# A hybrid decoder block on one core: expert rows added into the residual by the scatter, the last expert placed by TensorE, the gate matmul of the tail in split form, and the down bias and the per-layer embedding computed ahead of the experts

## The chip, the core and the metric

The kernel runs on one core of one Trainium2 chip. A core has TensorE (PE: matmuls, and PEld: its weight loads), VectorE (DVE), ScalarE (ACT), GpSimd (POOL) and SyncE (SP), and 16 DMA engines that all of them share. The metric is the device time of one execution in microseconds (us); lower is better. Times of a trace are counted from the start of the profiled span.

## The reference, cut to what matters

One decoder block over 512 tokens of width 1024 in float32: a mixer (not touched), then a mixture of experts (4 of 32 experts for each token), then a gated per-layer embedding and a final norm.

```python
# the mixture of experts, for each token t and its 4 experts e with softmax weights w
gu = h[t] @ w_gate_up[e] + b_gate_up[e]
gate, up = split(gu)            # clamped to 7
act = (up + 1) * gate * sigmoid(1.702 * gate)
out[t] += w * (act @ w_down[e] + b_down[e])

x = x + out
ple_gate = sigmoid(rms_norm(x, ple_norm_g) @ w_ple_gate)     # 1024 x 1024
x = x + ple_gate * (p @ w_ple_proj)                          # 256 x 1024
return rms_norm(x, final_norm_g)
```

## The kernel before, in words

The program is written out engine by engine, with semaphores between the engines; nothing is scheduled by a tool. It has three parts, which the trace puts at 0 to 660 us (the mixer), 660 to 1887 us (routing and 32 experts) and 1887 to 1996 us (the tail).

**Split matmuls.** A float32 product is made of three matmuls in the type fp32r: each operand is written as a high part (an ACT copy that rounds) and a low part (a DVE subtraction), and high x high, low x high and high x low are summed in PSUM. Plain float32 matmuls are used in the tail and for small products; each of them stands in the trace as two rows.

**Routing.** PE computes the logits (L1697), DVE picks the top 4 and builds one-hot rows, PE ranks the tokens of each expert (L1704, L1707). Then a loop over the 32 experts turns ranks into slots: DVE compares (L1398), PE multiplies the one-hot block with token numbers (L1801). The result is `tok_idx` (which token sits in slot s of expert e) and `dst_idx` (its row in the buffer `y_rows` of 2048 rows, one for each token and choice). While this loop runs, ACT makes the high parts of the first three weight chunks (L1023), and the DMAs of `wpg`, the 4 MB of gate weights, run (L1009).

**Experts.** Weights come as 12 chunks of 1 MB for each expert, by SP, into a ring of 6 buffers; a slot is loaded again when DVE has made its low part (L593, L600). Split parts have 3 buffers. For each expert POOL gathers the rows of its tokens from `h_rows` by an indirect DMA (L742), PE turns them (L1715), ACT and DVE split them into `xgT_h`, `xgT_l`; PE adds the gate/up bias by four short matmuls (L1720), multiplies 8 chunks into `gu_ps` (L1729, L1733), then adds the down bias by two matmuls (L1720, `down_bias`) and multiplies 4 chunks into `dn_ps` (L1744, L1749). ACT copies `dn_ps` into `y_sb` (L1035) and POOL scatters it into `y_rows` (L754). POOL's order in the loop is: wait for PE's turning, gather the rows of the expert three ahead, wait for `y_sb`, scatter, wait until the scatter has landed, and free `y_sb`.

**Passes.** After the 32 experts each engine runs through `passes` (L497), a loop that reads the largest expert's row count from SBUF three times, and would repeat the experts if one had more than 128 rows. None has here.

**Tail.** SP loads `p`, `w_ple_proj`, the residual `x1_rows` and the final gain, and after POOL's `moe_end` the 16 tiles of `y_rows` (L638). PE turns `p` and multiplies the embedding (L1835, L1842). For each of 4 blocks of 128 tokens DVE adds four weighted expert rows to the residual (L1499), ACT and DVE compute the norm (L1094, L1105, L1096, L1490), DVE scales the rows (L1504), PE turns them (L1855), DVE applies the gain (L1507), PE multiplies by the gate weights in plain float32 (L1862), ACT applies the sigmoid (L1091, L1092), DVE multiplies and adds (L1514, L1515), and a second norm gives the output rows (L1519), which SP stores (L641).

## Time and profile before

| what | us |
|---|---|
| runs: median of 3 (lowest to highest) | 2001.38 (2000.07 to 2005.04) |
| the profiled execution, device time | 1997.68 |
| its span in the trace | 1996.0 |
| PE busy in the span | 1879.9 (94%) |
| DVE busy | 1436.4 (72%) |
| ACT busy | 1154.7 (58%) |
| POOL busy | 301.8 (15%) |
| DMA moved | 512.41 MB, mean 257 GB/s |

Busy time is a share of the whole span; the stages differ. A granted TensorE clock of 1.00 in a stretch means 2.4 GHz throughout, 0.50 means 1.2 GHz throughout. A row of the timeline has the start in us, the length in us, the engine, the line, the operation, the tiles (output <- inputs), the count of merged instructions, and in brackets how long the engine had been idle and what ended that. Matmul rows overlap by their pipeline, so that the pace is read from one start to the next, not from the lengths.

### The profile page before, as it was taken

To read this page: it belongs to the slowest core of one execution; us is meant where nothing else is said; L and a number is where in the kernel's file an instruction comes from. 1 tells how busy PE (TensorE), PEld (TensorE's weight loads), DVE (VectorE), ACT (ScalarE), POOL (GpSimd) and SP (SyncE) were. 2 spreads that over 40 slices of the span, in tenths; PEclk is the share of its full clock that TensorE was granted. 3 is DMA by queue.
4 is the path that set the end of the run, shared out by engine and by line. 5 is a ranking of instruction groups with operands and counts; after the bars stand their busy time and mean duration, and the time that the engine had idled before them with its cause. 6 is when DMAs were issued, how large, how long until landed. Compare 5 with 4: busy or idle time off the path is not lost.

```text
span 1996.0 us, 25440 instructions
## 1 busy us (share of the span) xinstructions
PE 1879.9 (94%) x9038; PEld 1520.5 (76%) x9038; DVE 1436.4 (72%) x1021; ACT 1154.7 (58%) x898; POOL 301.8 (15%) x267
## 2 busy tenths in 40 slices
PE   6999998989999668999999999999999999999787
PEld 5788887768879556888888888888888888888633
DVE  3576585553341557898898988988889888898545
ACT  4555554242231236777777777777777777777423
POOL 5133323610000010111011110110101101010000
PEclk9999999999999678999999999999999999999989
DMA  5334434143364247999999999999999999999550
GB/s 171 104 105 117 108 119 114 56 132 97 94 196 174 105 184 279 357 367 369 361 364 362 371 365 366 371 366 376 362 363 371 358 370 367 359 369 357 195 210 38
DMA packets 155559, 512.41 MB, mean 257 GB/s; under 512 B 14964, under 2 KB 75028, under 8 KB 121876
## 3 DMA queue, kind: packets, MB, share of 16 engines
q1 hardware_dynamic: 141860, 482.26, 65.8%
q0 software_dynamic: 11520, 25.19, 4.2%
q10 hardware_dynamic: 2128, 4.26, 0.6%
q8 instruction: 34, 0.56, 0.1%
q14 instruction: 17, 0.14, 0.0%
HBM read 502.15 MB, written 26.28 MB: 265 GB/s over the span
## 4 chain that ended last, share of the span: by engine, by line
PE 81%; DVE 7%; ACT 5%; issue 3%; POOL 3%; DMA 1%; SPq 0%; DVEq 0%; ACTq 0%; POOLq 0%
PE gu_ps L1729 23%; PE gu_ps L1733 12%; PE dn_ps L1744 12%; PE gu_ps L1541 6%; PE gu_ps L1542 6%; PE gu_ps L1543 6%; PE dn_ps L1749 6%; PE et_ps L1715 3%; PE gu_ps L1862 2%; PE gu_ps L1720 1%; ACT w_hi L799 1%; POOL win L726 1%; PE gu_ps L1560 1%; PE gu_ps L1842 1%; PE dn_ps L1720 1%
## 5 line engine op out<-in xcount | busy, mean ns | idle before, releaser
L1427 DVE TENSOR_TENSOR split_l<-ring,split_h 128x2048 fp32r<-128x2048 f32 x384 | 871.6, 2290 | 133.9 <-ACT split_h L1023 129.6
L1023 ACT ACTIVATE split_h<-ring 128x2048 fp32r<-128x2048 f32 x384 | 731.1, 1917 | 187.6 <-PE gu_ps L1733 144.6
L1729 PE MATMUL gu_ps<-split_h,xgT_h 128*128 128x512 f32 x1024 | 285.1, 400 | 0.7 <-DVE xgT_l L1433 0.7
L1729 PE MATMUL gu_ps<-split_h,xgT_l 128*128 128x512 f32 x1024 | 275.9, 391 | 0.0
L1733 PE MATMUL gu_ps<-split_l,xgT_h 128*128 128x512 f32 x1024 | 274.8, 390 | 0.0
L1729 PEld LDWEIGHTS gu_ps<-split_h,xgT_l 128*128 128x128 f32 x1024 | 193.4, 189 | 41.3
L1733 PEld LDWEIGHTS gu_ps<-split_l,xgT_h 128*128 128x128 f32 x1024 | 193.1, 189 | 40.8
L1729 PEld LDWEIGHTS gu_ps<-split_h,xgT_h 128*128 128x128 f32 x1024 | 191.1, 189 | 41.7 <-DVE xgT_l L1433 1.6
L1111 DVE TENSOR_TENSOR w_lo<-w_raw,w_hi 128x2048 fp32r<-128x2048 f32 (+1 forms) x45 | 106.1, 2358 | 152.7 <-ACT w_hi L799 152.6
L1744 PE MATMUL dn_ps<-split_h,actT_h 128*128 128x512 f32 x512 | 167.7, 409 | 1.9 <-DVE actT_l L1433 1.9
L739 POOL COPY icur<-tok_idx 128x1 int32 (+1 forms) x32 | 39.9, 1247 | 800.7 <-PE et_ps L1715 757.7
L1744 PE MATMUL dn_ps<-split_h,actT_l 128*128 128x512 f32 x512 | 159.2, 392 | 0.0
L1541 PE MATMUL gu_ps<-hT_h,w_hi 128*128 128x512 f32 x392 | 154.9, 395 | 0.0
L1542 PE MATMUL gu_ps<-hT_l,w_hi 128*128 128x512 f32 x392 | 153.0, 390 | 0.0
L1543 PE MATMUL gu_ps<-hT_h,w_lo 128*128 128x512 f32 x392 | 152.9, 390 | 0.0
L1749 PE MATMUL dn_ps<-split_l,actT_h 128*128 128x512 f32 x512 | 137.2, 390 | 0.0
L799 ACT ACTIVATE w_hi<-w_raw 128x2048 fp32r<-128x2048 f32 (+1 forms) x45 | 85.0, 1889 | 59.6 <-PE gu_ps L1543 53.2
L1744 PEld LDWEIGHTS dn_ps<-split_h,actT_l 128*128 128x128 f32 x512 | 96.7, 189 | 20.8
L1749 PEld LDWEIGHTS dn_ps<-split_l,actT_h 128*128 128x128 f32 x512 | 96.3, 188 | 20.5
L1744 PEld LDWEIGHTS dn_ps<-split_h,actT_h 128*128 128x128 f32 x512 | 94.5, 190 | 22.7 <-DVE actT_l L1433 2.4
L1541 PEld LDWEIGHTS gu_ps<-hT_h,w_hi 128*128 128x128 f32 x392 | 74.1, 189 | 15.5 <-issue 0.6
L1543 PEld LDWEIGHTS gu_ps<-hT_h,w_lo 128*128 128x128 f32 x392 | 73.8, 188 | 15.5
(252 smaller groups left out, 2546.0 us busy)
## 6 DMA issues: line engine op xcount, KB each, us to landing
ring<-in_w_gate_up SPq DMA_DIRECT2D x256, 1024.0 KB, 7.0
ring<-in_w_down SPq DMA_DIRECT2D x128, 1024.0 KB, 7.5
w_raw<-in_w_in SPq DMA_DIRECT2D x28, 1024.0 KB, 5.8
arow<-acum_rows POOLq DMA_DIRECT2D x16, 512.0 KB, 6.6
w_raw<-in_w_ssd_out SPq DMA_DIRECT2D x8, 1024.0 KB, 5.7
yr<-y_rows SPq DMA_DIRECT2D x16, 512.0 KB, 10.4
w_raw<-in_w_in SPq DMA_DIRECT2D x9, 512.0 KB, 6.6
w_raw<-in_w_mix_out SPq DMA_DIRECT2D x4, 1024.0 KB, 8.8
```

Source lines behind the costliest of these rows:

```text
L799: a.activation(w_hi[HI_SLOT[n]][:, 0:size], w_raw[RAW_SLOT[n]][:, 0:size], ACT.Copy).then_inc(w_high, 1)
L1023: a.activation(split_h[s % SPLIT][:, :], ring[s % RING][:, :], ACT.Copy).then_inc(hi_done, 1)
L1111: v.tensor_tensor(w_lo[RAW_SLOT[n]][:, 0:size], w_raw[RAW_SLOT[n]][:, 0:size], w_hi[HI_SLOT[n]][:, 0:size].bitcast(F32), ALU.subtract).the ...
L1427: v.tensor_tensor(split_l[s % SPLIT][:, :], ring[s % RING][:, :], split_h[s % SPLIT][:, :].bitcast(F32), ALU.subtract).then_inc(lo_done, 1)
L1541: o = t.matmul(pb(key)[:, cols], sh, mh, start=n == 0, stop=False)
L1542: o = t.matmul(pb(key)[:, cols], sh, ml, start=False, stop=False)
L1543: o = t.matmul(pb(key)[:, cols], sl, mh, start=False, stop=n == len(parts) - 1)
L1715: o = t.transpose(et_ps[:, k * P:k * P + P], blocks[:, k * P:k * P + P], ident[:, :])
L1729: t.matmul(gu_ps[:, b * 512:b * 512 + 512], x[:, k, :], split_h[s][:, b * 512:b * 512 + 512], start=False, stop=False)
L1733: o = t.matmul(gu_ps[:, b * 512:b * 512 + 512], xgT_h[:, k, :], split_l[s][:, b * 512:b * 512 + 512], start=False, stop=k == KD - 1)
L1744: t.matmul(dn_ps[:, b * 512:b * 512 + 512], x[:, 2 * r + k, :], split_h[s][:, k * DM + b * 512:k * DM + b * 512 + 512], start=False, stop= ...
L1749: o = t.matmul(dn_ps[:, b * 512:b * 512 + 512], actT_h[:, 2 * r + k, :], split_l[s][:, k * DM + b * 512:k * DM + b * 512 + 512], start=Fal ...
```

## The change

1. **The scatter adds.** The DMA of POOL adds the rows of `y_sb` to `x1_rows`, the residual in DRAM, instead of writing them to `y_rows`. The routing weight is applied earlier, as the scale of ACT's copy into `y_sb`: the slot loop now yields the weight of each slot (`wslot`) beside the token, and POOL copies the next expert's column into `wcur` (`weigh`). `y_rows`, its loads and the 16 weighted additions in the tail are gone.
2. **The last expert** isn't scattered: its product stays in `dn_ps`, is scaled and split (`y_h`, `y_l`), and is placed by matmuls with a 0/1 matrix (`place`, slot against token) and added to the residual on DVE.
3. **The gate matmul of the tail** takes split operands: the weights with the norm's gain folded in (`wpg_h`, `wpg_l`), the unnormed rows (`x2T_h`, `x2T_l`), and the norm's factor becomes the scale of the sigmoid. The order is by k, so that the first block can start before all weights are split; the last block of 128 tokens is finished in two halves.
4. **The down bias** leaves the experts: `share3` holds each token's weight for each of the 32 experts, and share x `b_down` is added to the residual `X` once, by `add_bias`, after the slot loop. The stores of `x1_rows` wait for that.
5. **The embedding** p x w_ple_proj is computed between the routing's steps and in `add_bias`; its inputs are loaded during the last block of the mixer.

```diff
+                if c == CH - 1:
+                    wait_proj(sp, ("MO", c, 1))
+                    sp.dma_start(prow[:, :, :], p[0, 0].rearrange("(c p) d -> p c d", p=P)).then_inc(p_loaded, 16)
+                    sp.dma_start(pj[:, :, :], w_ple_proj[0].rearrange("(k p) f -> p k f", p=P)).then_inc(p_loaded, 16)
+                    for m in range(3):
+                        sp.dma_start(bdown[m * NE:m * NE + NE, :], b_down[0]).then_inc(bd_loaded, 16)
                 sp.dma_start(h_rows[c * P:c * P + P, :], h2[:, c, :]).then_inc(rows_stored, 16)
-                sp.dma_start(x1_rows[c * P:c * P + P, :], X[:, c, :]).then_inc(rows_stored, 16)
-
-            sp.wait_ge(rows_stored, 16 * 2 * CH)
+            sp.wait_ge(rows_stored, 16 * CH)
+            for c in range(CH):
+                sp.wait_ge(bd_added, c + 1)
+                sp.dma_start(x1_rows[c * P:c * P + P, :], X[:, c, :]).then_inc(x1_stored, 16)
             weights(0, RING)
...
-            sp.dma_start(prow[:, :, :], p[0, 0].rearrange("(c p) d -> p c d", p=P)).then_inc(p_loaded, 16)
-            sp.dma_start(pj[:, :, :], w_ple_proj[0].rearrange("(k p) f -> p k f", p=P)).then_inc(p_loaded, 16)
-            for c in range(CH):
-                sp.dma_start(x2[c][:, :], x1_rows[c * P:c * P + P, :]).then_inc(x2_loaded[c], 16)
             sp.dma_start(ogain[:, :], final_norm_g.partition_broadcast(P)).then_inc(ogain_loaded, 16)
             sp.wait_ge(moe_end, 1)
             for c in range(CH):
-                rows = y_rows[c * ROWS // CH:(c + 1) * ROWS // CH, :].rearrange("(p k) d -> p k d", k=TOPK)
-                for k in range(TOPK):
-                    sp.dma_start(yr[c][:, k, :], rows[:, k, :]).then_inc(yr_loaded[c][k], 16)
-            for c in range(CH):
-                sp.wait_ge(o_done, c + 1)
...
+            def scatter(n, col, steps, following=None):
                 pool.wait_ge(y_evac, n + 2)
                 alone(pool)
+                if following is not None:
+                    weigh(following)
...
-                g.indirect_dma_start(out=y_rows, out_offset=bass.IndirectOffsetOnAxis(ap=dcur[:, 0:1], axis=0),
+                g.indirect_dma_start(out=x1_rows, out_offset=bass.IndirectOffsetOnAxis(ap=dcur[:, 0:1], axis=0),
+                                     in_=y_sb[:, :], in_offset=None, bounds_check=SEQ - 1,
+                                     oob_is_err=False, compute_op=ALU.add
                                      ).then_inc(y_stored, 16)
...
-            act.wait_ge(rows_stored, 16 * 2 * CH)
-            for h in range(2):
-                act.dma_start(wpg[h][:, :, :], wpg_v[:, :, h * 512:h * 512 + 512]).then_inc(pg_loaded, 16)
+            for k in range(0, KD, 4):
+                act.dma_start(wpg[:, k:k + 4, :], wpg_v[:, k:k + 4, :]).then_inc(pg_loaded, 16)
+            embed(0)
+            act.wait_ge(share_done, 1)
+            act.wait_ge(bd_loaded, 16 * 3)
+            a.activation(bstk[:, :], bdown[:, :], ACT.Copy).then_inc(b_high, 1)
+            act.wait_ge(share_turned, 1)
+            a.activation(shareT[:, :], bank[4][0:3 * NE, :], ACT.Copy).then_inc(share_high, 1)
+            embed(1)
+            act.wait_ge(rows_stored, 16 * CH)
...
-                a.activation(y_sb[:, :], dn_ps[:, :], ACT.Copy).then_inc(y_evac, 1)
+                act.wait_ge(w_ready, n + 1)
+                a.activation(y_sb[:, :], dn_ps[:, :], ACT.Copy, scale=wcur[:, 0:1]).then_inc(y_evac, 1)
...
+                if isinstance(j, int):
+                    for i in range(2, 2 * CH):
+                        embed(i)
...
-            def down_bias(n, e):
+            def down_free(n):
 
                 pe.wait_ge(y_evac, n + 1)
-                for b in range(2):
-                    bias(dn_ps[:, b * 512:b * 512 + 512], e, 2 * DM + b * 512)
 
...
+            def add_bias():
...
+                pe.wait_ge(share_low, 1)
+                pe.wait_ge(slots_done, 2)
+                for c in range(CH):
+                    if c >= 2:
+                        pe.wait_ge(bd_added, c - 1)
+                    ps = dn_ps if c % 2 == 0 else et_ps
+                    for h in range(2):
+                        o = t.matmul(ps[:, h * 512:h * 512 + 512], shareT[:, c * P:c * P + P],
+                                     bstk[:, h * 512:h * 512 + 512], start=True, stop=True)
+                    o.then_inc(bd_mm, 1)
+                    embed(4 + c)
+                pe.wait_ge(pp_read, 2 * CH + 1)
+                pe.wait_ge(bd_added, CH)
+
...
+            t.transpose(et_ps[:, 0:P], ident[:, :], ident[:, :]).then_inc(last_mm, 1)
+
+            def put_back(c):
...
+                for h in range(2):
+                    pe.wait_ge(y_low, h + 1)
+                    for n, part in enumerate((y_h, y_l)):
+                        o = t.matmul(tail_b[c][:, h * 512:h * 512 + 512], place[:, c * P:c * P + P],
+                                     part[:, h * 512:h * 512 + 512], start=n == 0, stop=n == 1)
+                o.then_inc(back_mm, 1)
...
+            def gate(c, k, h):
+
+                if c == 0 and h == 0:
+                    pe.wait_ge(pg_low, k + 1)
+                ps = bank[2 * ((c + 1) % 2) + h]
+                for n, (a, b) in enumerate(((x2T_h, wpg_h), (x2T_l, wpg_h), (x2T_h, wpg_l))):
+                    o = t.matmul(ps[:, :], a[c % 2][:, k, :], b[:, k, h * 512:h * 512 + 512],
+                                 start=k == 0 and n == 0, stop=k == KD - 1 and n == 2)
+                return o
...
```

Where the rows stand now. **ACT between the exponential of the routing and the first expert.** Before (`split_h` is the high part of a weight chunk, `xgT_h` the turned rows):

```order
L1002 ACTIVATE rt_78<-rt_78 128x16 [waits route_in]
L1009 DMA wpg_187<-in_w_ple_gate 128x8x512 [waits rows_stored,logits_mm]
L1009 DMA wpg_188<-in_w_ple_gate 128x8x512
L1023 ACTIVATE split_h_167<-ring_161 128x2048 [waits chunk_used,e_loaded0]
L1023 ACTIVATE split_h_168<-ring_162 128x2048 [waits chunk_used,e_loaded1]
L1023 ACTIVATE split_h_169<-ring_163 128x2048 [waits chunk_used,e_loaded2]
L1015 ACTIVATE xgT_h<-et_ps 128x1024 [waits et_done]
```

Now (`pp` is a half block of the embedding, `bstk` the bias, `shareT` the turned weights of the tokens):

```order
L1047 ACTIVATE rt_77<-rt_77 128x16 [waits route_in]
L1058 DMA wpg<-in_w_ple_gate 128x4x1024 [waits logits_mm]
L1058 DMA wpg<-in_w_ple_gate 128x4x1024
L1052 ACTIVATE pp<-gu_ps 128x512 [waits pp_mm]
L1062 ACTIVATE bstk<-bdown 96x1024 [waits bd_loaded,share_done]
L1064 ACTIVATE shareT<-et_ps 96x512 [waits share_turned]
L1052 ACTIVATE pp<-gu_ps 128x512 [waits pp_mm]
L1080 ACTIVATE split_h_166<-ring_160 128x2048 [waits chunk_used,e_loaded0,rows_stored]
L1080 ACTIVATE split_h_167<-ring_161 128x2048 [waits chunk_used,e_loaded1]
L1080 ACTIVATE split_h_168<-ring_162 128x2048 [waits chunk_used,e_loaded2]
L1052 ACTIVATE pp<-gu_ps 128x512 [waits pp_mm] x6
L1072 ACTIVATE xgT_h<-et_ps 128x1024 [waits et_done]
```

The first three high parts stand behind `shareT` now, which waits for PE's turning after the slot loop; before, only the DMA issues stood between them and the exponential.

**DVE between the slot loop and the first expert's rows.** Now; before, the three `split_l` stood right behind the slot sums, and `xgT_l` right behind them:

```order
L1512 TENSOR_TENSOR wslot<-rt_78,dn_ps 128x32 [waits slot_step]
L1581 TENSOR_TENSOR bstk<-bdown,bstk 32x1024 [waits b_high]
L1584 TENSOR_TENSOR shareT<-et_ps,shareT 32x512 [waits share_high]
L1529 TENSOR_TENSOR split_l_169<-ring_160,split_h_166 128x2048 [waits hi_done]
L1529 TENSOR_TENSOR split_l_170<-ring_161,split_h_167 128x2048 [waits hi_done]
L1529 TENSOR_TENSOR split_l_171<-ring_162,split_h_168 128x2048 [waits hi_done]
L1546 TENSOR_TENSOR X<-X,dn_ps 128x1024 [waits bd_mm]
L1546 TENSOR_TENSOR X<-X,et_ps 128x1024 [waits bd_mm]
L1546 TENSOR_TENSOR X<-X,dn_ps 128x1024 [waits bd_mm]
L1546 TENSOR_TENSOR X<-X,et_ps 128x1024 [waits bd_mm]
L1535 SCALAR_TENSOR_TENSOR xgT_l<-et_ps,xgT_h 128x1024 [waits et_hi]
```

Four additions to the residual `X` have come in between the low parts and the rows of the first expert.

**PE after the last expert.** Now (`et_ps<-ident` is a turning whose only use is to mark that PE has come this far; before, the first row here was the turning of `p`, behind the same branch):

```order
L1914 MATMUL dn_ps<-split_l_171,actT_h 128x512 x3
L529 UNCONDITIONAL_BRANCH
L527 REGISTER_ALU
L527 COMPARE_AND_BRANCH
L2021 MATMUL et_ps<-ident 128x128
L2032 MATMUL gu_ps<-y_h,place 128x512 [waits y_low,placed]
L2032 MATMUL gu_ps<-y_l,place 128x512
L2032 MATMUL gu_ps<-y_h,place 128x512 [waits y_low]
L2032 MATMUL gu_ps<-y_l,place 128x512
```

The mark on which ACT's `y_h` waits stands behind the loop `passes`, not in front of it.

## Rows read from the trace of the kernel before

**Rows 1.** Windows: span, busy us (count) of PE, PEld, DVE, ACT, POOL, clock, DMA.
```profile
679.00:705.00 26.00, 17.91 (x127) 13.18 (x127) 20.54 (x31) 1.83 (x2) 0.00 (x0) 0.50 0.31 114
1000.00:1200.00 200.00, 200.00 (x932) 162.64 (x931) 177.61 (x90) 148.21 (x90) 27.27 (x24) 1.00 0.96 365
```

**Rows 2.** Timeline of PE where one expert's gate/up chunks end.
```profile
887.99 1.07 PE L1733 MATMUL gu_ps<-split_l,xgT_h 128*128 128x512 f32 x4
888.90 0.61 PE L1720 MATMUL dn_ps<-bparts,sel 96*128 96x512 bf16 x2
889.15 0.82 PE L1744 MATMUL dn_ps<-split_h,actT_h 128*128 128x512 f32 x2
889.81 0.62 PE L1744 MATMUL dn_ps<-split_h,actT_l 128*128 128x512 f32 x2
```

**Rows 3.** Groups of DVE from 800 to 1840 us: busy, mean ns, idle before.
```profile
L1427 DVE TENSOR_TENSOR split_l<-ring,split_h 128x2048 fp32r<-128x2048 f32 x349 | 792.1, 2290 | 103.6 <-ACT split_h L1023 99.8
```

**Rows 4.** DMA view, 1000 to 1200 us: totals; issues with us to landing.
```profile
DMA packets 14027, 72.94 MB, mean 365 GB/s; under 512 B 2029, under 2 KB 2029, under 8 KB 8220
...
ring<-in_w_gate_up SPq DMA_DIRECT2D x44, 1024.0 KB, 7.0
...
y_rows<-y_sb,dcur POOLq DMA_INDIRECT x6, 7.7
```

**Rows 5.** DMA view, 800 to 850 us: GB/s in 40 slices.
```profile
GB/s 226 285 347 331 374 367 213 328 318 246 377 439 433 400 413 413 419 413 419 380 269 413 341 400 351 305 419 324 419 387 338 403 384 416 282 282 387 252 393 383
```

**Rows 6.** Timeline of POOL in one expert: gather's copy, scatter's issue.
```profile
896.18 1.28 POOL L739 COPY icur<-tok_idx 128x1 int32 x1 [24.46 <-PE et_ps L1715]
...
906.51 1.01 POOL L754 DMA_INDIRECT y_rows<-y_sb,dcur  x1 [0.88 <-POOL dcur L751]
```

**Rows 7.** Timeline from the logits to the first expert's second chunk.
```profile
661.76 3.60 PE L1697 MATMUL et_ps<-wr,h2T 128*128 128x32 f32 x16 [0.78 <-ACT h2T L999]
...
668.76 1.04 DVE L1365 TENSOR_REDUCE chosen<-oh 128x128 f32<-128x512 f32 x1
...
674.14 1.89 PE L1707 MATMUL dn_ps<-chosen,ones 128*128 128x32 f32 x8
...
675.32 5.51 ACT L1023 ACTIVATE split_h<-ring 128x2048 fp32r<-128x2048 f32 x3 [1.18 <-issue]
...
705.27 0.29 DVE L1402 COPY slotv<-dn_ps 128x128 f32<-128x128 f32 x1 [0.88 <-PE dn_ps L1801]
...
706.89 2.10 POOL L739 COPY icur<-tok_idx 128x1 int32<-128x1 int32 x1 [42.99 <-DVE dst_idx L1409]
...
718.71 1.97 PE L1715 MATMUL et_ps<-ident,xg 128*128 128x128 f32 x8 [13.47 <-DMA xg<-h_rows,icur]
...
723.04 2.07 PE L1729 MATMUL gu_ps<-split_h,xgT_h 128*128 128x512 f32 x4 [0.67 <-DVE xgT_l L1433]
...
727.76 1.09 PE L1729 MATMUL gu_ps<-split_h,xgT_h 128*128 128x512 f32 x4
```

**Rows 8.** Line L497 (`passes`): PE's loads: ns min/median/max, first and last start.
```profile
L497 PEldq TENSOR_LOAD <-maxcount x3: 308/316/488, 1883.1 to 1889.6; - x3
```

**Rows 9.** Timeline of the tail.
```profile
1885.62 1.07 PE L1749 MATMUL dn_ps<-split_l,actT_h 128*128 128x512 f32 x4
...
1897.44 15.87 PE L1842 MATMUL gu_ps<-pj,pT 128*128 128x512 f32 x32 [1.11 <-ACT pT L1079]
...
1905.77 5.25 DVE L1499 SCALAR_TENSOR_TENSOR x<-yr,wts,x 128x1024 f32<-128x1024 f32 x4 [22.90 <-DMA yr<-y_rows]
```

**Rows 10.** Timeline of PE, the last block's gate matmuls.
```profile
1970.99 14.00 PE L1862 MATMUL gu_ps<-wpg,h3T 128*128 128x512 f32 x32 [0.94 <-DVE h3T L1507]
```

**Rows 11.** Timeline of DVE, its last row.
```profile
1991.56 1.28 DVE L1519 SCALAR_TENSOR_TENSOR o_sb<-x,rstd,ogain 128x1024 f32<-128x1024 f32 x1
```

**Rows 12.** Groups of the tail: busy, mean ns, idle before.
```profile
L1096 ACT ACT_TABLE_LOAD x5 | 6.4, 1283 | 0.1
...
L1515 DVE TENSOR_TENSOR x<-x,gt 128x1024 f32<-128x1024 f32 x4 | 4.9, 1224 | 0.1
```

457 lines of the change are left out of this document (303 added, 154 removed).

## The prediction, made before the changed kernel had run

> **What bounds the kernel now.** I read the windows first. From 1000 to 1200 us PE is busy for 200.00 of 200.00 us at a clock of 1.00, DVE for 177.6, ACT for 148.2 [rows 1]; so the expert stage has the pace of PE's instruction stream, and what leaves that stream leaves the time, as long as nobody else falls behind. The timeline of PE shows that stream without a hole: four matmuls of 512 columns take 0.91 us from start to start, and the two bias matmuls stand in it like any others [rows 2]. Then I read the two places where PE is not full: between logits and first expert, where from 679 to 705 us the clock is 0.50, which is 1.2 GHz, and DVE and PE hand one small block to and fro [rows 1, 7]; and the tail, 109 us long, where the embedding, the loads of `y_rows` and the plain float32 gate matmuls follow one another [rows 9, 10]. The time has three terms accordingly: experts, front, tail.
>
> **Experts: the down bias.** The chunk before starts its last four matmuls at 887.99, the bias follows at 888.90, and the fourth matmul behind it starts 0.91 us after it, at 889.81; so two bias matmuls cost half of 0.91, 0.455 us [rows 2]. They stand in the full stream for 31 experts; for the last one PE waits for ACT and DVE anyway. 31 x 0.455 = 14.1 us off. Nothing is put into PE's stream in their place; ACT's copy into `y_sb` only gets a scale.
>
> Who could fail to follow a period of 35.36 us instead of 35.81? DVE idles 103.6 us in 29 experts, 3.6 us in each [rows 3], so 0.455 less leaves 3.1. POOL adds a copy of one column; its copy of such a column takes 1.28 us, and it has 24.5 us of idle time in front of each gather [rows 6]. Queued behind the added copy are the scatter's index copy and the scatter; the one who needs them is ACT's next copy into `y_sb`, a period later. The wait `w_ready` is met as long before. The stores of the residual are waited for only ahead of the first `y_sb`.
>
> The DMA is the question. It moves 365 GB/s [rows 4], 13.07 MB in 35.81 us. 2048 rows of 4 KB over 32 experts are 0.26 MB in one scatter, and an addition must read as much again: 13.33 MB in 35.36 us is 377 GB/s. The slices of a shorter window reach 413 to 439 GB/s [rows 5], and a weight load lands 7.0 us after its issue [rows 4], while its slot is one of six, wanted some 15 us later (six chunks of 2.72 to 2.98 us, less the splitting). So I take nothing for it. The trace has no adding DMA. From below nothing excludes that it lands as the plain one does, 7.7 us [rows 4]; upwards I bound it by the plain one and a gather behind one another, 15.2 us. Either is hidden among the experts: the scatter is issued at 906.51 and POOL's next gather comes 35.81 us after the one at 896.18, so about 25 us stay. A gain isn't excluded for the plain write either, but has no way to the end.
>
> The Trainium skill ("Perfetto Trace Analysis", Roofline) puts the ceiling of one core's 16 DMA engines at about 435 GB/s. By that rule 377 fits; by the share of 0.96 that the window shows [rows 1] the queues are already full. The slices near 435 side with the rule, and no run here shows more.
>
> **Front.** Up to 665.4 us (logits end, 661.76 + 3.60) nothing changes; the loads of `p` and the bias are issued while PE still works on the mixer. PE then waited until DVE had `chosen` at 669.8; now it turns `p` and makes a half block of the embedding. One half block is 4 rows; the 32 rows of the old embedding take 15.87 us, partly at 1.2 GHz [rows 9], so 1.7 us at the high and 3.4 at the low clock. With 2.0 for the turning and 1.0 for ACT's copy it ends at 670 to 672: 0 to 2 us late. The counts (ended at 676.0) follow. After them DVE has 1 us less to do (the softmax moved ahead), PE one half block more. I put the slot loop at +0.5, between -1.5 and +2.7. The token list is ready after two small operations instead of six, 1.0 us earlier; with that the first gather lands at 718.2 instead of 718.7.
>
> But the first expert no longer hangs on the gather. ACT's three high parts (5.51 us, ended 680.8 before, in the shade of the slot loop [rows 7]) now come after `shareT`: 707.7 to 713.2. DVE's three low parts, 2.29 us each, end at 716.4, and four additions of 1.22 us [rows 12] follow, the last two also waiting for PE: PE has four turnings, six half blocks and eight bias matmuls from 705.3 on, of which the first two half blocks are at the low clock; its last bias product comes at 720.4 and the last addition ends at 721.7. The last half block and its copy end at 722.8. So the rows are turned at 722.9 instead of 718.7: +4.2, +0.5 for the slot loop. Against it: before, PE came out of 13.47 us of idleness [rows 7] and took 4.72 us for the first chunk (723.04 to 727.76), where 2.72 is the warm pace; now it comes out of matmuls, which gives back about 2.0, and 0.5 in the turning. Sum +2.2 us, with -1 if the slots gain and +8 if all of PE's inserted work stays at the low clock. SP is held up too: its seventh weight load stands behind the stores that wait for the additions, 722.5 instead of 709.0; it lands by 733 and is wanted at 738. That costs nothing, with 5 us to spare. Removed weight conversion on POOL at the start was not on a path.
>
> **Tail.** PE's last chunk ends at 1886.5 (1885.62 + 0.91). Now `passes` lies in the path: PE's third load of the count starts at 1889.6 [rows 8], so the marker comes at 1890.9. Before it was hidden behind the load of `p`. Then two half copies of ACT (0.6 each, half of a pass of 1.2 us), two of DVE, four matmuls cold: the first block is placed at 1894.0, the second at 1895.7; DVE adds (1.22) by 1895.4, PE turns it by 1897.7, ACT and DVE split it by 1900.1. The residual must be there at 1894: POOL's scatter of expert 30 has landed at 1882, POOL's own `passes` ends at 1886.2, SP issues at 1888; at 400 GB/s the first block is there at 1892.5, so up to 1.5 us of extra landing time are free, and the upper bound of 15.2 us would cost 4.
>
> From 1900.2 PE goes through four gate blocks: each 48 matmuls at 0.227 us (0.91 / 4) = 10.9 us instead of 14.00 [rows 10], and 1.0 for the turning in three of them: 43.6 + 3.0, to 1946.8. DVE, which splits the eight gate weights (1.28 each) between four additions in block 0, delivers the last at 1909.1, when PE reaches it at 1910.7: close, without a price. ACT switches tables twice a block, 1.28 each [rows 12]; its chain per block (copy, square, two tables, roots, sigmoid) is about 12 us, as long as PE's 11.9, and ends up some 2 us behind it. The last block in halves: sigmoid, two products, square, table, root, output in halves of 0.65 us, to 1956.0. From the last output's end (1992.84) to the span's end it was 3.2 us [rows 11]. New end: 1959.0 against 1996.0 in the same frame: 37.0 off. Bounds: 30 (late residual, cold first gate block, ACT as the limit) to 41.
>
> **Sum.** -14.1 + 2.2 - 37.0 = -48.9. Against the profiled execution's own 1997.68 (span 1996.0 and 1.7 around it) that is 1948.8. The median of the runs is 3.7 above that execution, 2001.38, and the new runs will be compared with it: 2001.4 - 48.9 = 1952.5. Its own range is 1943 to 1962.
>
> **Rivals.**
> A second: *the weight stream becomes the bound of the experts*. For it: the DMA share 0.96 in the window. Against it: the slices above 413 and no idle time of PE or ACT before a landing. If the period just stays, the 14.1 are lost: 1966.6. If 365 GB/s is all there is, 13.33 MB take 36.5 us, 0.7 more than before in each of 31 experts: 1966.6 + 22 = 1988.6.
> A third: *the tail keeps half of its length in hand-overs*. For it: `passes`, copies, products and additions alternate over four engines between 1886 and 1900, each at an estimate, and ACT's chain is as long as PE's; any slip of 3 us a block moves the end by 12. With the front at its upper bound (+8) and the tail at 25: -14.1 + 8 - 25 = -31, 1970.
> A fourth, slower than before: *the adding scatter outlasts the period*. Its place is POOL's wait for the landing, then ACT's copy into `y_sb`, behind which the next high part is queued, and PE behind that. It decides from 32.5 us of landing time on (issue 906.5, ACT's next copy at 939), and makes the kernel slower from 34.1 us on, 30 times the excess being more than 48.9: over four times the plain 7.7. At 36 us it would be 1952.5 + 30 x 3.5 = 2057. For it: rows must be read, added and written, in a queue among full ones. The Trainium skill ("Collectives: The Full Stack", Stop ④) says that the adder in the DMA path makes a reduction read, read, write, with the addition itself free; by that the fourth case is out. No row here shows it.
>
> **How the numbers follow.** Forecast 0.70, weight stream 0.12, long tail 0.13, slow scatter 0.05. The predicted time is the forecast's, 1952.5. The range takes the forecast's, the third case and the lower part of the second: 1943 to 1975. A measurement of this kernel can tell 0.3%, 6 us. All of the first three cases lie more than 6 us below 2001: faster 0.94, same 0.01, slower 0.05.
>
> **What would show it.** Right: PE still fully busy among the experts with 35.36 us from expert to expert; the first rows turned at 722 to 725 with DVE's additions ending just before; `y_h` starting about 4.5 us after PE's last chunk; gate blocks 11.9 us apart; a landing time of the adding DMA below 15 us. Wrong: idle time of ACT before `split_h` put down to a DMA (second case); gate blocks more than 13 us apart, or PE waiting for the residual's load (third); POOL's gather late and ACT waiting before `y_sb` (fourth).

## The result, and the profile after

The median of the kernel after is 1947.49 us (1942.71 to 1955.84, 4 runs), of the kernel before on the same chip 2000.72 us (1997.56 to 2005.04, 4 runs). The ratio is 0.9736, 95% interval 0.9709 to 0.9763: faster, by 2.6%. The forecast was 1952.5 us, its own range 1943 to 1962, the range with the rivals 1943 to 1975. The profiled execution took 1946.32 us, its span is 1944.6 us, 51.4 us shorter than the one of before.

The duration of the mixer, ahead of every changed step, differs by several us from run to run (the logits' end lies between 660.6 and 667.4 us in the traces below). So I compare the stretches between five fixed points: the logits' end; the second expert's gate/up bias matmuls; the start of PE's last four matmuls of the experts; the first gate matmul of the tail; the span's end.

| stretch | before | after | change | predicted |
|---|---|---|---|---|
| start to logits' end (mixer) | 665.36 | 664.73 | -0.6 | 0 |
| A: front and first expert | 89.58 | 89.55 | 0.0 | +2.2 |
| B: experts | 1130.68 | 1116.21 | -14.5 | -14.1 |
| C: end of experts to first gate matmul | 34.09 | 15.75 | -18.3 | -19.5 |
| D: gate blocks to the end | 76.29 | 58.36 | -17.9 | -17.5 |

The windows of after, columns as in [rows 1]:

```profile
679.00:705.00 26.00, 18.41 (x125) 13.44 (x125) 20.41 (x35) 0.42 (x1) 0.18 (x1) 0.55 0.11 44
1000.00:1200.00 200.00, 200.00 (x928) 163.89 (x927) 178.82 (x91) 150.05 (x92) 33.94 (x30) 1.00 0.98 368
```

PE is as full among the experts as before, DMA share and GB/s have risen (0.96 to 0.98, 365 to 368). The DMA view of 1000 to 1200 us answers to [rows 4]:

```profile
DMA packets 14360, 73.61 MB, mean 368 GB/s; under 512 B 2047, under 2 KB 2047, under 8 KB 8703
...
ring<-in_w_down SPq DMA_DIRECT2D x24, 1024.0 KB, 8.5
...
x_rows<-y_sb,dcur POOLq DMA_INDIRECT x6, 9.5
```

The adding scatter lands after 9.5 us (plain 7.7, predicted 7.7 to 15.2). POOL's rows of one expert answer to [rows 6]:

```profile
893.62 1.75 POOL L770 COPY icur<-tok_idx 128x1 int32 x1 [23.27 <-PE et_ps L1879]
...
904.13 1.59 POOL L791 DMA_INDIRECT x_rows<-y_sb,dcur  x1 [0.89 <-POOL dcur L788]
```

The bytes answer to the prediction's 13.33 MB and 377 GB/s: the profile counts 368 GB/s, 13.0 MB in a period of 35.36 us, and 385.10 MB from 800 to 1840 us, against 385.18 MB in the same window of a run whose scatter only writes (d2, below). So the 0.26 MB that the prediction added for the reading of the old rows doesn't show in these counts.

POOL stays ahead: 23.27 us of idleness before the gather's copy, and the scatter, issued at 904.13, has some 25 us to land. DVE's splitting of weights [rows 3] now shows 96.3 us of idleness in 354 low parts (before 103.6 in 349).

The front, from the timeline, answers to [rows 7]:

```profile
661.14 3.59 PE L1843 MATMUL et_ps<-wr,h2T 128*128 128x32 f32 x16 [0.78 <-ACT h2T L1041]
...
673.52 1.06 PE L1870 MATMUL dn_ps<-chosen,ones 128*128 128x32 f32 x8
...
677.42 0.97 PE L1988 MATMUL dn_ps<-tokv,onehot 128*128 x8
...
718.44 1.22 DVE L1546 TENSOR_TENSOR X<-X,et_ps 128x1024 f32<-128x1024 f32 x1 [0.74 <-PE et_ps L1974]
...
720.81 1.09 PE L1879 MATMUL et_ps<-ident,xg 128*128 128x128 f32 x8 [0.69 <-ACT pp L1052]
...
727.13 1.07 PE L1893 MATMUL gu_ps<-split_h,xgT_h 128*128 128x512 f32 x4
```

(The first three rows are PE's alone, the others all engines'.) The last count matmuls end sooner relative to the logits than before (x8 in 1.06 us instead of 1.89 in [rows 7]: PE at 2.4 GHz, not 1.2). DVE's last addition starts at 718.44, the rows are turned at 720.81, 56.1 us after the logits' end (53.4 before), and the second chunk starts at 727.13.

And the tail, answering to [rows 8 to 10]:

```profile
1870.49 1.07 PE L1914 MATMUL dn_ps<-split_l,actT_h 128*128 128x512 f32 x4
...
1876.59 0.47 PE L2021 MATMUL et_ps<-ident 128*128 128x128 f32 x1 [5.04 <-issue]
1877.10 1.26 ACT L1166 ACTIVATE y_h<-dn_ps,wcur 128x512 fp32r<-128x512 f32 x2 [4.53 <-PE et_ps L2021]
...
1882.27 1.55 PE L2042 MATMUL et_ps<-ident,x 128*128 128x128 f32 x8
...
1886.24 0.47 PE L2051 MATMUL gu_ps<-wpg_h,x2T_h 128*128 128x512 f32 x1 [0.59 <-issue]
...
1891.83 1.03 PE L2042 MATMUL dn_ps<-ident,x 128*128 128x128 f32 x8
...
1903.70 1.03 PE L2042 MATMUL et_ps<-ident,x 128*128 128x128 f32 x8
```

PE sits idle for 5.04 us before the marker (L2021), because its sequencer is in the loop `passes` (t1 below shows what takes the time there); then copy, product, addition, turning and split follow one another to the first gate matmul at 1886.24. The turnings of the next blocks stand 11.87 us apart, as predicted (11.9).

### The profile page after: what moved, and what is told of

Its sections match the earlier page's. It is cut to its first block, busy times and chain, and to the rows that moved or that the text cites. A ratio compares the mean times of both kernels' runs of the same rounds, so it can differ in the third digit from the quotient of the medians.

```text
span 1944.6 us, 25546 instructions
## 1 busy us (share of the span) xinstructions
PE 1855.0 (95%) x9067; PEld 1529.1 (79%) x9067; DVE 1427.2 (73%) x1012; ACT 1168.0 (60%) x912; POOL 323.8 (17%) x297
## 4 chain that ended last, share of the span: by engine, by line
PE 83%; DVE 6%; ACT 5%; issue 3%; POOL 3%; DMA 0%; SPq 0%; DVEq 0%; ACTq 0%; POOLq 0%
PE gu_ps L1893 24%; PE dn_ps L1908 12%; PE gu_ps L1897 12%; PE gu_ps L1687 6%; PE gu_ps L1688 6%; PE gu_ps L1689 6%; PE dn_ps L1914 6%; PE et_ps L1879 3%; PE gu_ps L1884 1%; PE gu_ps L2051 1%; ACT w_hi L841 1%; PE gu_ps L1706 1%; POOL win L757 1%; DVE w_lo L1208 1%; DVE split_l L1529 1%
## 5 line engine op out<-in xcount | busy, mean ns | idle before, releaser
L770 POOL COPY icur<-tok_idx 128x1 int32 (+1 forms) x32 | 51.9, 1621 | 765.5 <-PE et_ps L1879 727.2
L1908 PE MATMUL dn_ps<-split_h,actT_h 128*128 128x512 f32 x512 | 161.4, 397 | 4.7 <-issue 4.7
## 6 DMA issues: line engine op xcount, KB each, us to landing
wpg<-in_w_ple_gate ACTq DMA_DIRECT2D x2, 2048.0 KB, 10.9
```

The costliest lines, as they stand in the source:

```text
L1908: t.matmul(dn_ps[:, b * 512:b * 512 + 512], x[:, 2 * r + k, :], split_h[s][:, k * DM + b * 512:k * DM + b * 512 + 512], start=r == 0 and k ...
```

## The experiments

All are edits of the kernel after; the ratio is to the kernel before, run on the same chip. Stretches in us:

| run | median | ratio, 95% interval | A | B | C | D |
|---|---|---|---|---|---|---|
| after | 1947.49 | 0.9736 (0.9709 to 0.9763) | 89.55 | 1116.21 | 15.75 | 58.36 |
| d1_bias_back | 1956.45 | 0.9794 (0.9768 to 0.9820) | 89.69 | 1130.57 | 15.17 | 58.41 |
| d2_plain_scatter | 1947.93 | 0.9739 (0.9718 to 0.9760) | 89.63 | 1116.29 | 15.31 | 58.34 |
| d3_gate_plain | 1954.27 | 0.9773 (0.9750 to 0.9796) | 89.59 | 1116.26 | 15.56 | 66.43 |
| d4_last_scattered | 1956.64 | 0.9789 (0.9766 to 0.9811) | 89.71 | 1116.27 | 23.22 | 59.86 |
| f1_no_embedding | 1946.28 | 0.9733 (0.9707 to 0.9758) | 92.17 | 1114.36 | 14.94 | 58.35 |
| t1_one_count_load | 1942.64 | 0.9709 (0.9685 to 0.9734) | 89.64 | 1116.29 | 12.02 | 58.39 |
| t2_gate_one_product | 1939.19 (one run) | - | 89.70 | 1116.31 | 15.74 | 50.32 |
| d5_extra_copy | 1967.77 | 0.9828 (0.9802 to 0.9854) | 89.56 | 1136.82 | 15.69 | 58.35 |
| w1_warm_slots | 1948.36 | 0.9734 (0.9707 to 0.9760) | 91.47 | 1114.83 | 15.04 | 58.36 |
| f2_front_reordered | 1944.98 | 0.9728 (0.9695 to 0.9762) | 87.66 | 1114.95 | 16.00 | 58.42 |
| t3_turn_at_end | 1960.44 (one run) | - | 89.60 | 1116.28 | 15.60 | 72.38 |
| b1_both | 1938.15 | 0.9684 (0.9654 to 0.9713) | 87.75 | 1114.96 | 10.22 | 58.39 |

Where nothing in it is touched, a stretch repeats within 0.2 us (A, B and D; C lies between 14.9 and 16.0, which goes with the length of one branch of PE's sequencer, see t1), so the stretches show what the medians, with an interval of 5 us to either side, can't. One exception: in the four runs with another front (f1, w1, f2, b1) B is 1.3 to 1.9 shorter, in the two places where PE comes out of a wait (7.1 us ahead of the second expert's bias, 0.7 to 1.2 shorter behind it; 4.7 us ahead of the last expert's down chunks, 0.5 to 0.6 shorter) and runs at 1.2 GHz for a while. The length of that while differs between runs; what sets it wasn't settled.

**The bias back in the experts (d1).**

```diff
...
-            def down_free(n):
+            def down_free(n, e):
                 pe.wait_ge(y_evac, n + 1)
+                for b in range(2):
+                    bias(dn_ps[:, b * 512:b * 512 + 512], e, b * 512)
```

> Of the kernel after, the two bfloat16 bias matmuls are put back in front of each expert's down chunks (columns of the gate bias stand in for the down bias, so the output has a wrong bias; the work is the old one). Theory 1, PE's stream bounds the experts: 31 x 0.455 = +14 us, the period goes from 35.36 back to 35.81, PE fully busy, total about 1961.5. Rival, the weight stream bounds: the period stays at 35.36, the total at 1947.5, and the matmuls fall into idle time of PE.

B grew by 14.4 us and nothing else changed by more than it varies: theory 1 holds. The gate/up bias matmuls of the experts stand 35.84 us apart instead of 35.36, so the down bias is worth 0.48 us in each of 31 experts, 14.9 us. In the last expert it is worth nothing, as the prediction had it; there the time goes the other way by 0.6 us. The last four matmuls of the last expert's first down chunk, in the kernel after:

```profile
1861.80 1.57 PE L1914 MATMUL dn_ps<-split_l,actT_h 128*128 128x512 f32 x4
```

and in d1:

```profile
1876.41 1.09 PE L1914 MATMUL dn_ps<-split_l,actT_h 128*128 128x512 f32 x4
```

From the last turning to the experts' last four matmuls it takes 17.97 us in the kernel after and 17.41 in d1 (17.36 before). With the bias PE has two waits, of 2.19 and 1.85 us, ahead of this chunk and is back at its full pace with the matmuls shown; without it one wait of 4.70 us, and they still run slow. That the bias in the gap is the reason is not shown: the four runs with another front have no bias there either and take 17.4 us.

**A scatter that only writes (d2).**

```diff
-                                     oob_is_err=False, compute_op=ALU.add
+                                     oob_is_err=False
```

> Of the kernel after, the scatter writes instead of adding (the residual is overwritten; wrong values, same rows). Theory 1, the adding scatter is hidden: landing time from 9.5 back to about 7.7 us, total unchanged, 1947.5 (within 2 us). Rival, its read competes with the weights: the period falls below 35.36 and the total by 3 us or more. Rival, it is an end of the tail: the residual's load starts up to 2 us sooner and the first gate block with it.

The DMA view of d2, 1000 to 1200 us (issues, KB each, us to landing):

```profile
x_rows<-y_sb,dcur POOLq DMA_INDIRECT x6, 7.8
```

The landing time is back at 7.8 us, A to D stay as they were: the addition costs 1.7 us of landing time and nothing of the kernel's time; this is theory 1, and neither rival. C is 0.4 shorter, within what C varies by.

**One more MB for each expert (d5)**, to measure how near the second rival was.

```diff
                     if more:
+                        act.wait_ge(gmix_loaded, n0 * 16 + e * 16 + 16)
+                        act.dma_start(extra_rows, w_gate_up[0, 0, 0:P, :]).then_inc(gmix_loaded, 16)
                         high(j, e, 15)
```

> Of the kernel after, ACT issues in each of 30 experts one more DMA of 1 MB, a copy of weights within device memory that nobody waits for except the next such copy. Theory 1, there is room in the DMA: 374 + 30 = 404 GB/s are moved, the period stays 35.36, landing times grow to 8 to 11 us, total within 5 us. Rival (the second one of the prediction), the queues are full at a share of 0.98: 14.4 MB at the same GB/s take 38.1 us, +2.8 us in 30 experts, +83 us.

Neither held. B is 20.6 us longer, 0.69 for each of the 30 copies. The window of 1000 to 1200 us in d5:

```profile
1000.00:1200.00 200.00, 197.76 (x909) 158.79 (x909) 176.24 (x91) 147.00 (x90) 57.63 (x30) 1.00 1.00 390
```
Its DMA view of the same stretch:

```profile
ring<-in_w_gate_up SPq DMA_DIRECT2D x44, 1024.0 KB, 11.6
ring<-in_w_down SPq DMA_DIRECT2D x22, 1024.0 KB, 14.4
```
And a row of ACT from the timeline:

```profile
916.92 1.92 ACT L1081 ACTIVATE split_h<-ring 128x2048 fp32r<-128x2048 f32 x1 [1.33 <-DMA ring<-in_w_gate_up]
```

At a DMA share of 1.00 the 16 engines move 390 GB/s, the weights land after 11.6 to 14.4 us (7.1 and 8.5 in the kernel after), and ACT now waits for them. It isn't the issuing of the copy that costs: the first five periods with a copy keep 35.36 us, while the landing of the weights grows (median 9.2 us from 760 to 860 us, 12.9 from 960 to 1060), and only from 971 us on the periods are 35.9 to 36.8. So there is a ceiling at 390 for this mix, 6% above the 368 of the kernel after: the mechanism of the second rival is real and stood 22 GB/s away. The slices of 413 to 439 [rows 5] were peaks of a changing load and not a rate that can be kept up; the 435 GB/s of the Trainium skill ("Perfetto Trace Analysis", Roofline) weren't reached here either, as a mean over 200 us.

**Plain gate matmuls (d3).**

```diff
-                for n, (a, b) in enumerate(((x2T_h, wpg_h), (x2T_l, wpg_h), (x2T_h, wpg_l))):
-                    o = t.matmul(ps[:, :], a[c % 2][:, k, :], b[:, k, h * 512:h * 512 + 512], ...
+                o = t.matmul(ps[:, :], x2T_h[c % 2][:, k, :].bitcast(F32),
+                             wpg_h[:, k, h * 512:h * 512 + 512].bitcast(F32), ...
```

> Of the kernel after, each of the 64 gate products of the tail is one plain float32 matmul of the high parts instead of three fp32r matmuls (splitting work stays). Theory 1, PE bounds the gate blocks: 4 x (14.0 - 10.9) = +12.4 us, blocks 15.0 us apart instead of 11.9, total about 1960. Rival, ACT's and DVE's chain of about 12 us per block is the bound: blocks become 15 apart all the same only if PE is alone; with a chain that was already later than PE, the gain would be smaller, +6 to +10.

PE's timeline in d3, the second and the third turning:

```profile
1893.32 1.04 PE L2042 MATMUL dn_ps<-ident,x 128*128 128x128 f32 x8
...
1907.92 1.04 PE L2042 MATMUL et_ps<-ident,x 128*128 128x128 f32 x8
```

Turnings are 14.60 us apart instead of 11.87, D is 8.1 us longer: 1.4 ahead of the first of these turnings, two times 2.73, and only 1.2 behind the last, where the kernel after ends with a chain over ACT and DVE (sigmoid, product, addition, square, roots) that started while PE was still at the last block (from PE's last gate matmul to the end it is 9.3 us in d3, 11.9 in the kernel after). So each theory has a half: PE sets the distance of the blocks, as theory 1 says, with 14.6 us instead of its 15.0, and the sum is the rival's. The split is worth 8 of the 17.9 us of D, not 12.

**One product instead of three (t2)** asks who comes next behind PE.

```diff
-                for n, (a, b) in enumerate(((x2T_h, wpg_h), (x2T_l, wpg_h), (x2T_h, wpg_l))):
+                for n, (a, b) in enumerate(((x2T_h, wpg_h),)):
```

> Of the kernel after, the gate uses the high x high products alone: 16 matmuls per block instead of 48 (less accurate gate). Theory 1 of the prediction, ACT's chain per block is about 12 us and as long as PE's: blocks stay 11 to 12 us apart, the end within 3 us. Rival, counted by rows of the trace: sigmoid 1.26, product 1.22, addition 1.23, square 1.25, two tables 2.56 and roots make 9 us: 7 to 9 us gained. Second rival, PE alone is the bound: 4.7 us a block, 25 us gained.

ACT's timeline in t2, the sigmoids of the first two blocks:

```profile
1898.25 1.27 ACT L1181 ACTIVATE gt<-gu_ps,rstd 128x512 f32<-128x512 f32 x2
...
1908.28 1.27 ACT L1181 ACTIVATE gt<-gu_ps,rstd 128x512 f32<-128x512 f32 x2
```

With PE's work down to a third D falls by 8.0 us, and the sigmoids stand 10.0 us apart (1898.25, 1908.28). So the chain of ACT and DVE, with the splitting of the next block's rows in it, takes 10 us a block; my "about 12" was too long, and with 11.87 it is PE that sets the distance of the blocks in the kernel after. The first rival of the two has it.

**The turning at the end of a block (t3).**

```diff
-                        if k == 3:
+                        if k == KD - 1:
                             turned_x2(c + 1)
```

> Of the kernel after, PE turns the next block of the tail after the last gate product of a block instead of after the fourth k. Theory 1, the place of the turning is worth the hand-over over ACT and DVE, 1.02 + 1.23 and gaps, 2.4 us in each of three blocks: turnings 14.2 us apart instead of 11.9, the end 7 us later. Rival, ACT's chain is the bound anyway: under 3 us.

PE's timeline in t3, the start of the second block:

```profile
1900.89 0.77 PE L2051 MATMUL gu_ps<-wpg_h,x2T_h 128*128 128x512 f32 x1 [2.47 <-DVE x2T_l L1611]
1901.45 0.63 PE L2051 MATMUL gu_ps<-wpg_h,x2T_l 128*128 128x512 f32 x1
```

D is 14.0 us longer, twice what I expected. The wait is the expected 2.47 us, but behind it the matmuls follow at 0.43 us (the next row is at 1901.88) until they are back at 0.23, from 1904.0 on: idle for 2.5 us, PE comes back at 1.2 GHz. The step from turning to turning is 16.06 us, 4.2 more than 11.87: 2.5 of waiting and 1.7 of slow clock. The second wait, 2.47 us before 1916.96, is followed by eight slow matmuls too. The third is not:

```profile
1933.16 0.50 PE L2051 MATMUL gu_ps<-wpg_h,x2T_h 128*128 128x512 f32 x1 [2.44 <-DVE x2T_l L1611]
```

Behind 2.44 us of waiting the last block runs at 0.23 us a matmul from its second matmul on (1933.50), so a wait of this length costs 2.5 or 4.2 us, and these rows don't say which. PE's last matmul comes 11.3 us later by all this. The other 2.8 us of D lie behind it: the chain over ACT and DVE to the end takes 14.7 us there instead of 11.9. One run only; but 14.0 is far beyond the 0.1 us by which D varies. The turning in the middle of the block is thus worth more than the split.

**The last expert scattered (d4).**

```diff
+            scatter(NE - 1, tok_idx[:, NE - 1:NE], 2 * NE)
             pool.sem_inc(moe_end, 1)
...
-            for h in range(2):
-                ... y_h[:, at] ... y_high
+            a.activation(y_sb[:, :], dn_ps[:, :], ACT.Copy, scale=wcur[:, 0:1]).then_inc(y_evac, 1)
```

> Of the kernel after, the last expert's rows go through y_sb and the adding scatter like the others, and the residual is loaded behind it; no y_h, y_l, no products with the selection matrix, no DVE additions. Theory 1: from the end of ACT's copy a scatter (index copy and issue 2, landing 9.5), a load (about 4), a turning and a split (about 3.5) follow one another: first gate block at 1897 instead of 1886.2, +11 us, total about 1958. Rival: the gain of the put-back is small because copies, products and additions cost nearly as much as the scatter: +4 or less.

The timeline of d4: the last scatter, the residual's loads, the first gate matmul:

```profile
1875.62 1.55 POOL L791 DMA_INDIRECT x_rows<-y_sb,dcur  x1 [0.89 <-POOL dcur L788]
1881.88 1.77 SPq L669 DMA_DIRECT2D x<-x_rows  x4
...
1889.84 0.77 PE L2045 MATMUL gu_ps<-wpg_h,x2T_h 128*128 128x512 f32 x1 [2.42 <-DVEq L1605]
```

C is 7.5 us longer and D 1.5 (PE starts the first block at 1.2 GHz after two waits). Placing the last expert on chip is worth 9.0 us, not 11: with the queues empty the same adding scatter lands 6.1 us after the start of its issue, where it takes 9.5 among the weights. Two more traces have such a scatter with the queues otherwise empty: an adding one in the kernel after, issued at 1858.0, landed after 6.0 us, a writing one in the kernel before, issued at 1873.7, after 3.2. So adding instead of writing costs 2.8 us of landing time alone and 1.7 among the weights.

**One load of the count (t1).**

```diff
-            with eng.Fori(1, PASSES) as j:
-                rows = eng.value_load(maxcount[0:1, 0:1], min_val=0, max_val=SEQ)
-                with eng.If(rows > j * P):
-                    yield j
+            more = eng.value_load(maxcount[0:1, 0:1], min_val=0, max_val=SEQ)
+            with eng.If(more > P):
+                with eng.Fori(1, PASSES) as j:
+                    ... (as before)
```

> Of the kernel after, the loop over further passes is entered only when the count exceeds 128: one load of the count and one branch per engine instead of three. Theory 1, PE's sequencer in this loop is what holds the marker: it goes from 6.1 us after the start of PE's last four matmuls (1870.49 to 1876.59) to about 2, y_h, the first gate block and the span's end come 4 us sooner. Rival, the residual's load or ACT's gate weights are right behind: 1 to 2 us.

Line L529 (`passes`) of the kernel after, the branches of PE's sequencer (min/median/max in ns, first and last start):

```profile
L529 PEldq COMPARE_BRANCH  x3: 221/221/4105, 1869.1 to 1876.1; - x3
```
PE's timeline in t1, the last four matmuls and the marker:

```profile
1873.29 1.07 PE L1917 MATMUL dn_ps<-split_l,actT_h 128*128 128x512 f32 x4
1876.20 0.33 PE L2024 MATMUL et_ps<-ident 128*128 128x128 f32 x1 [1.84 <-issue]
```

One of PE's three branches takes 4.1 us in the kernel after. It is the first, and it was there before, and it is still there in t1. Line L498 of the kernel before and line L528 of t1:

```profile
L498 PEldq COMPARE_BRANCH  x3: 221/227/3420, 1884.1 to 1890.4; - x3
```
```profile
L528 PEldq COMPARE_BRANCH  x1: 4550/4550/4550, 1871.6 to 1871.6; - x1
```

This branch starts before PE's last four matmuls (at 1884.1 against 1885.62 before, at 1871.6 against 1873.29 in t1) and so stands mostly in their shade. In all the runs it takes 3.4 to 4.8 us and ends 1.8 to 3.4 us behind the start of the last four matmuls. What t1 took out is what came after it, the rest of the three rounds: 3.4 us in the kernel after (1873.2 to 1876.5). With one round the marker starts 2.91 us behind the last four matmuls instead of 6.10, and C is 3.7 us shorter: the marker was held by the sequencer, as the prediction had it, and nothing else stood right behind it. Wherever there is a marker it starts within 0.1 us of the end of the last branch, so the end of the first one is what C varies by.

**Front without the embedding (f1).**

```diff
-            embed(0)
...
-            embed(1)
...
-                embed(2)
-                embed(3)
...
-                    embed(4 + c)
-                pe.wait_ge(pp_read, 2 * CH + 1)
```

> Of the kernel after, the eight half blocks of the embedding (PE matmuls and ACT copies) are left out; p is still loaded and turned, pp is a constant. Theory 1, the embedding's work costs the front next to nothing, since DVE's lows and additions end only a little before it and its matmuls lift PE's clock: rank matmuls back at 1.2 GHz (6 us instead of 3.2), rows turned 1.7 us sooner, first chunk slower again by 1 to 2 us; logits end to second expert within 2 us of the kernel after (89.6 us). Rival, the embedding stands on the path with most of its matmul time: logits end to second expert 6 to 10 us shorter.

Two windows of f1:

```profile
665.00:679.00 14.00, 7.96 (x38) 7.31 (x36) 10.68 (x33) 3.58 (x4) 2.69 (x1) 0.50 0.55 207
...
705.00:725.00 20.00, 9.60 (x26) 5.31 (x25) 15.07 (x14) 7.01 (x5) 3.20 (x5) 0.50 0.46 159
```
The same two of the kernel after:

```profile
665.00:679.00 14.00, 12.34 (x53) 7.58 (x52) 11.43 (x36) 4.18 (x5) 0.69 (x1) 0.64 0.59 219
...
705.00:725.00 20.00, 17.01 (x47) 8.19 (x46) 13.96 (x10) 10.43 (x12) 2.92 (x4) 0.90 0.47 166
```

A is 2.6 us longer without the work than with it. The clock says why: 0.50 throughout, where the kernel after has 0.64 and 0.90. The rows are turned 0.7 us sooner, but the counts take longer, so that the slot loop ends 1.5 us later, and the first expert starts at 1.2 GHz: from the turning of its rows to its second chunk it takes 9.6 us instead of 6.3. B is 1.9 shorter, from the second expert's start (37.0 us to the next bias matmuls instead of 38.2); the sum of A and B is 0.8 longer. Moved here the embedding costs nothing: theory 1. Without it PE waits for DVE's last addition (1.32 us) ahead of the turning, 15.2 us behind the turning of `share`.

**More matmuls in the slot loop (w1)**, since f1 seemed to say that work pays for itself.

```diff
                         o.then_inc(onehot_used, 1)
+                        t.matmul(bank[3][:, :], slotrow[:, :], tokv...[:, 0:512], start=True, stop=True)
```

> Of the kernel after, PE makes one more bfloat16 matmul of 512 columns, into a bank that nobody reads, behind each of the 32 slot products. Theory 1 (from the run without the embedding: extra matmuls lift the granted clock and so pay for themselves): clock of the slot loop from 0.55 up to 1.0, the loop from 1.64 us a pair down to DVE's 1.4, share's turning and the two half blocks behind it (1.08 and 5.98 us) down to 0.9 and 3.6, rows turned 5 to 7 us sooner after logits end than 56.1. Rival, the loop's own extra matmuls stand in the way of the hand-over: 0.2 to 0.4 us more a pair at an unchanged clock of 0.5, rows turned 3 to 6 us later.

The slot loop's window in w1:

```profile
679.00:705.00 26.00, 25.36 (x155) 13.91 (x155) 20.39 (x36) 0.00 (x0) 0.18 (x1) 0.57 0.13 52
```

PE was busy for 25.36 of 26 us, and still the mean clock stood at 0.57: at 1.2 GHz for most of it. The loop kept its pace (26.3 us, 26.0 in the kernel after), since the added matmuls fit beside DVE's comparisons. Behind it the first two half blocks did come faster, in 4.28 us instead of 5.98, but then PE waited 2.50 us for DVE's addition (0.80 in the kernel after), and the next half block took 3.46 us instead of 1.88 (A +1.9). Neither theory held. Why the embedding's matmuls raise the clock and these don't stays open.

**The front in another order (f2).**

```diff
                 embed(2)
-                embed(3)
...
-                    embed(4 + c)
-                pe.wait_ge(pp_read, 2 * CH + 1)
+                    embed(3 + c)
+                embed(7)
...
                 for i in range(3):
                     low(j, 0, i - UP)
+                    if isinstance(j, int):
+                        for c in ((0, 1), (2, 3), ())[i]:
+                            ... (wait for bd_mm, X += ps)
```

ACT's `high` for the first three chunks stands ahead of its copies of `bstk` and `shareT`, and PE's wait for `pp_read` behind the first `rows_in`.

> Of the kernel after, ACT's three high parts come ahead of shareT, DVE's four additions stand between its low parts, PE's second half block of the two behind share's turning comes after the first bias products, and the wait for ACT's last copy of pp comes behind the turning of the rows. Theory 1, PE's own work (16.3 us from share's turning) sets the turning of the rows: 16.0 us after share's turning instead of 17.35, -1.3 us. Rival (my step in the prediction: ACT's highs and DVE's lows and additions set it): 3 us or more sooner.

The timeline of f2: share's turning, DVE's last addition, the turning of the rows:

```profile
703.69 1.08 PE L1959 MATMUL et_ps<-ident,share 128*96 128x128 f32 x4
...
715.88 1.22 DVE L1544 TENSOR_TENSOR X<-X,et_ps 128x1024 f32<-128x1024 f32 x1
...
719.00 1.04 PE L1877 MATMUL et_ps<-ident,xg 128*128 128x128 f32 x8
```

The rows are turned 15.3 us after share's turning (17.35 in the kernel after), with DVE's last addition long done (715.88 + 1.22): PE's own work is the limit, theory 1, by a little more than I gave it. A is 1.9 us shorter. In the kernel after PE's work had two waits in it, 0.80 us for DVE's addition and 0.69 for ACT's copy; f1 shows DVE's chain, with 15.2 us, right behind.

**Both (b1).** 

> The edits of t1_one_count_load and f2_front_reordered together. Theory, the two places are apart and their gains add: logits end to second expert 87.7 us instead of 89.55, last four matmuls of the experts to the span's end 70.4 us instead of 74.1, together 5.6 us off the kernel after: about 1942 us, ratio 0.971. Rival: one of them is only the run's own scatter (the first expert's slow stretch of PE varies by about 1 us between runs): 2 to 4 us off.

The median is 1938.15 us, ratio 0.9684 (0.9654 to 0.9713), 9 us below the kernel after; this version beats both. By the stretches A gives 1.8, C 5.5, B 1.3, more than the 5.6 expected. Part of that is luck: one round of the loop left the marker 2.91 us behind the last four matmuls in t1 and 2.03 here, with a first branch that ended sooner. PE's timeline in b1, from the last four matmuls to the first gate matmul:

```profile
1868.09 1.07 PE L1915 MATMUL dn_ps<-split_l,actT_h 128*128 128x512 f32 x4
1870.12 0.33 PE L2023 MATMUL et_ps<-ident 128*128 128x128 f32 x1 [0.97 <-issue]
...
1873.24 0.40 PE L2034 MATMUL gu_ps<-y_h,place 128*128 128x512 f32 x1
1873.48 0.40 PE L2034 MATMUL gu_ps<-y_l,place 128*128 128x512 f32 x1
...
1878.31 0.47 PE L2053 MATMUL gu_ps<-wpg_h,x2T_h 128*128 128x512 f32 x1 [0.58 <-issue]
```

The marker comes 2.03 us behind the last four matmuls, and the clock doesn't fall: the products with `place` stand 0.23 us apart (0.43 in the kernel after from 1878.72 on) and the turning takes 1.09 instead of 1.55. So the shorter wait gave more than its own length, as the longer one in t3 cost more.

## Why the prediction was right, point by point

The four stretches are 50.8 us shorter, 48.9 were predicted. The misses are 0.4, 2.2 and 0.4 us to the good and 1.2 to the bad, so no large ones cancel. The median came out 5.0 us below the forecast; the other 3.1 of that are the mixer and the scatter of the medians, which the interval of 5 us covers.

- **Experts, -14.1 predicted, -14.5 found.** Reading the price of the bias from the distance of matmul starts in a full stream was right (d1). The miss of 0.4 is made of two: 0.03 us more in each of 31 periods, 0.9, and the last expert, rightly exempted, which took 0.6 longer at the low clock.
- **The adding scatter.** Taken as free with 7.7 to 15.2 us of landing; 9.5 found, no price (d2). The fourth rival is out by a factor of three. That the Trainium skill ("Collectives: The Full Stack", Stop ④) calls the addition itself free fits with what the kernel's time shows; the landing is 1.7 us longer.
- **The DMA as a bound.** Not the bound, but for a weaker reason than I gave. The "no idle time before a landing" was the sound argument; the slices above 413 weren't. With 390 as the ceiling (d5), the 13.0 MB that the profile counts in a period need 33.4 us of the 35.36 (13.33 MB, which no count shows, would need 34.2).
- **Front, +2.2 predicted, 0.0 found.** The rows were turned 2.7 us later than before instead of 4.2 + 0.5. The failed step is "I put the slot loop at +0.5": counted from the logits' end the loop's first product came 1.0 us and its last 1.2 us sooner than before, 1.7 better than I had it. The embedding's half block ahead of the counts brought PE to 2.4 GHz there; without it the counts are back at 1.2 GHz and the loop ends 1.5 us later (f1). The cause I named for the delay (ACT's highs behind `shareT`, then DVE's lows and additions) was not the last one, if by little: PE's own 16 us are (f2, and f1 for the 15.2 of the other). What the warm clock gives back, 2.5 predicted, came (2.7).
- **End of the experts, -19.5 predicted, -18.3 found.** `passes` lies in the path as said (t1). From the end of the last chunk to `y_h` it took 5.7 us instead of 4.5: the first branch of the loop ended 2.7 us behind the start of the last four matmuls, where it was 1.9 in the trace of before, and `y_h` starts 0.5 us behind the marker. From `y_h` to the first gate matmul it took 9.1 us, 9.2 predicted. Of the 18.3 us the put-back in place of the last scatter gives 7.5 (d4). The rest is argued from rows of before. The timeline of the kernel before:

```profile
1913.84 1.05 ACT L1094 ACTIVATE junk<-x 128x1024 f32<-128x1024 f32 x1
...
1917.63 1.30 PE L1855 MATMUL et_ps<-ident,h 128*128 128x128 f32 x8 [4.32 <-DVE h L1504]
...
1919.71 16.68 PE L1862 MATMUL gu_ps<-wpg,h3T 128*128 128x512 f32 x32 [0.78 <-DVE h3T L1507]
...
1936.23 1.04 PE L1855 MATMUL et_ps<-ident,h 128*128 128x128 f32 x8
...
1952.57 1.09 PE L1855 MATMUL et_ps<-ident,h 128*128 128x128 f32 x8 [0.36 <-DVE h L1504]
```

  The four weighted additions of the first block end at 1911.0 (1905.77 + 5.25 in [rows 9]), ACT's copies of the embedding keep its first square waiting until 1913.84, and the norm stands ahead of the turning. Between the kernel before and d4 lie 10.9 us: 5.3 for the additions, 2.8 for the embedding, 3.8 for the norm and 1.3 for an earlier start, less 2.3, because from the turning to the first gate matmul it now takes 4.4 us instead of 2.1. No run took these apart.
- **Gate blocks, -17.5 predicted, -17.9 found.** The new time was summed rightly, 46.6 us of PE and the chain behind it. What the split is worth was not: "10.9 us instead of 14.00" makes 3.1 a block, 12.4 in all, and 8.1 were found (d3). The 14.00 is the length of a row, while from start to start 32 plain matmuls take 13.6 us, so a block gains 2.7; and behind the last block the chain over ACT and DVE takes back 2.7. The other 9.8 us are argued from rows: in the kernel before the first block ran 2.7 us longer than the others (16.68 against 14.00), the turnings stood 18.60 and 16.34 us apart (14.60 in d3), and the chain behind the last gate matmul was 2.3 us longer. How dear a wait for the turning is, t3 shows: 14 us for three.
- **The third rival** ("ACT's chain is as long as PE's") rested on 12 us for a chain that takes 10 (t2).
